# RWKV side work of the middle pairs four places earlier, VectorE's scan and gates two steps later beside head seven

## The chip, the cores and the metric

The kernel runs on one core of one Trainium2 chip. The metric is the device time of one execution in microseconds (us); lower is better. Engines are named PE (TensorE, the matmuls), DVE (VectorE), ACT (ScalarE), POOL (GpSimd) and SP (SyncE, which here only issues transfers). Each engine works through its own instructions strictly in the order in which the program lists them and waits on semaphores where it needs another engine's result.

## The reference

One layer of a streaming encoder, 1024 positions of width 1024, in float32:

```python
h = x
proj = rms_norm(h, mix_norm) @ w_in_first
att = mla_group(proj[..., :MLA_COLS], ...)            # 8 heads, chunk-causal softmax attention
rw, _ = rwkv7_group(token_shift(proj[..., MLA_COLS:], mu), ...)   # 8 heads of 64
h = h + concatenate([att, rw]) @ w_out
h = h + mem_cross_attention(rms_norm(h, ca_norm), mem_n, ca_wq, ca_wkv, ca_wo)
h = h + squared_relu_mlp(rms_norm(h, mlp_norm), mlp_w_up, mlp_w_down)
return rms_norm(h, final_norm)
```

The part that matters here is the recurrence inside `rwkv7_group`, which runs strictly forward in time for each head:

```python
sa = einsum('bhvk,bhk->bhv', state, at)
state = state * wt[:, :, None, :] + sa[..., None] * bt[:, :, None, :] + vt[..., None] * kt[:, :, None, :]
y = einsum('bhvk,bhk->bhv', state, rt)
```

The decay `wt`, the removal vector `at`, its partner `bt` and the mixed key `kt` are made from the projection by low-rank products, tanh, exp, a norm over each head and a running sum of the log decay over time. Afterwards each head's `y` is normalized, gets a bonus term and is multiplied by a gate.

## The kernel before

**Stages.** The projection comes first, then the eight attention heads (outer loop `h` over heads, inner loop `q` over eight query windows of 128), then the RWKV loop, then the output projection, cross-attention and the MLP. Head seven is `h == BESIDE`, that is `h = 6`.

**RWKV loop.** The eight RWKV heads are worked in four pairs, `p = 0` to 3 (the text calls them first to fourth pair). In a pair the 1024 positions are 16 chunks of 64 in four groups `g`. A group begins with `solve` (PE L1433), `local` and `carry` (L1455 to L1492), and then has four steps `k`, one for each chunk `c`: PE makes the next state (`st`, L1512), DVE copies it out of PSUM (L2856), and PE makes the outputs (L1525). State `c + 1` needs the copy of state `c`. At the head of a group, the states need `mt`, a DVE sum (L2846). Also in the steps, PE works ahead for the next group: `double_q`, `double_z` (L1408 to L1422, with DVE's L2819 and L2828 behind them), `scores` (L1366, L1368, DVE's L2702 behind them), `tokens` (L1379 to L1382, ACT's copies behind them) and at the end `a_v` (L1395), which needs the state copy of the group's last chunk.

**Side work.** Between these steps stands side work: `prep(p + 1)`, which makes the next pair's inputs, and `post(p - 1)`, which finishes the previous pair's output. Each is cut into numbered slots; a slot may have instructions on PE, ACT and DVE. The RWKV loop has numbered places, 4 to 47 in each pair: places `11g + 4` to `11g + 6` stand in the head of group `g`, places `11g + 7 + 2k` and the one after it in step `k`. Before the change place `s` does slot `s`, and places 44 to 47 do slots 0 to 3 of the pair after next:

```python
def place_of(p, s):
    return (p, s) if s < SLOTS else (p + 1, s - SLOTS)
```

`beside(p, s)` on PE, ACT and DVE calls this. POOL and SP have their own order.

**Slots by name (DVE line in brackets).** 0 and 2: low-rank products on PE (L1237), tanh on ACT. 3: `kk`, `t1p` and the scan `L` (L2584, L2587, L2592). 4: `na`, `am` (L2595, L2598). 5: `k2` (L2601), and on ACT the squares `kksq` (L1964). 6 and 7: head sums on PE (L1240, in later pairs L1247), their logarithms on ACT (L1970, L1974). 10 to 12: exponentials on ACT. 14: `nkk` (L2604). 15: `at` (L2609). 16: `b`, `bt` (L2614, L2618). 17: `kt` (L2621). 18 and 19: `al` on PE (L1303), which needs `bt`, and its copy on DVE (L2631). 21: `rk` (L2638). 24: two memsets. 26 to 30: the substitution, 30 small operations in a chain (L2654, L2657) and a copy. 33 and 34: bonus sums (PE L1247, DVE L2667, L2671). `post` is 22 slots later: 24 the squares and 28 the head sums of y, 37 `yn`, `yb`, 38 and 39 the gate (PE L1237, DVE L2696).

**The transfer chain.** When slot 19 is done, SP stores the `al` blocks to HBM and loads them back as `sc_s`; the substitution waits for that load. After it SP stores the result and loads it into `H`; the next pair's first `double_q` (PE L1408) waits for that. SP's `inverse` and `blocks` issue these in a fixed order.

**Head seven.** Beside each `q` of heads seven and eight stand slots of `prep(0)`; `beside_heads` lists them. DVE does them after the maximum (`row_max`, L2534) of that `q`; the next `q`'s maximum comes after them. ACT's exponential and PE's transposes (L1182) wait for the maximum.

Of the kernel before, what the change touches and what calls it, by code (L numbers as in the profile page):

```python
# [19 lines left out]
NW = S // P  # L20
# [11 lines left out]
PAIRS = 4  # L32
# [84 lines left out]
BESIDE = 6  # L117
SLOTS = 44
POST = 22
RP_SET = 6  # L120
# [48 lines left out]
def build(nc, x_t, mem_t, pos, wall, vecs, con_d, headw, wv_d, lora_d, out_t):  # L169
    with ExitStack() as ctx:  # L170
# [291 lines left out]
        for g in range(SLOT_END):  # L462
            n, part, j = part_of(g)
# [124 lines left out]

        def place_of(p, s):

            return (p, s) if s < SLOTS else (p + 1, s - SLOTS)

        def beside_heads(h, q):

            i = 9 * (h - BESIDE) + q
            if h < BESIDE:
                return ()
            if i < 9:
                return ((0,), (1,), (2,), (3, 4), (5, 6), (7, 8, 9), (10, 11), (12, 13, 14), (15, 16, 17))[i]
            return ((), (18,), (19, 21, 22), (24,), (26, 27), (28, 29, 30), (33,), (34,), ())[i - 9]  # L600

        mm_act, mm_dve, mm_pe = sem("mem_act"), sem("mem_dve"), sem("mem_pe")
# [356 lines left out]
        def _(pe):  # L959
# [569 lines left out]
            def beside(p, s):  # L1529
                p, s = place_of(p, s)  # L1530
                if p == PAIRS:
                    return
                if p >= 1:
                    post(p - 1, s - POST)
                else:
                    attention_end(s)
                if p < PAIRS - 1:
                    prep(p + 1, s)
                elif s == 9:
                    memory_sums()  # L1540
# [292 lines left out]
        def _(act):  # L1833
# [209 lines left out]
            def beside(p, s):  # L2043
                p, s = place_of(p, s)
                if p == PAIRS:
                    return
                if p >= 1:
                    post(p - 1, s - POST)
                if p < PAIRS - 1:
                    prep(p + 1, s)  # L2050
                else:
                    memory_step(s)
# [334 lines left out]
        def _(dve):  # L2387
# [182 lines left out]
            def prep(n, s):  # L2570
# [10 lines left out]
                if s == 3:  # L2581
                    if n >= 1:
                        r_at(P_ACT, f"afirst_{n - 1}")
                    r(nc.vector.tensor_scalar(rKK, kk_, vec[:, V_KK + n:V_KK + n + 1], -1.0, ALU.mult, ALU.mult), "kk")  # L2584
                if s == 3:
                    r_at(P_ACT, f"tw1_{n}")
                    r(nc.vector.tensor_scalar(rT1, rT1, 1.0, None, ALU.add), "t1p")  # L2587
                if s == 3:
                    own("t1p")
                    if n == 0:  # L2590
                        dve.wait_ge(step_made, 3)
                    r(nc.vector.tensor_tensor_scan(rWi, rStep, rT1, 0.0, ALU.mult, ALU.add), "L")  # L2592
                if s == 4:
                    r_at(P_ACT, f"ta1_{n}")
                    r(nc.vector.tensor_scalar(rA, rA, -0.5, -0.5, ALU.mult, ALU.add), "na")  # L2595
                if s == 4:
                    own("na")
                    r(nc.vector.tensor_scalar(rT1, rA, 1.0, vec[:, V_KA + n:V_KA + n + 1], ALU.add, ALU.mult), "am")  # L2598
                if s == 5:
                    own("am")  # L2600
# [105 lines left out]
            def beside(p, s):  # L2706
                p, s = place_of(p, s)
                if p == PAIRS:
                    return
                if p >= 1:  # L2710
# [61 lines left out]
            for h in range(MLA_HEADS):  # L2772
                for q in range(NW):
# [9 lines left out]
                    if q < NW - 1:  # L2783
                        filled(h, q)
                        for s in beside_heads(h, q):
                            prep(0, s)
                if h < MLA_HEADS - 1:
                    queries(h + 1)
                filled(h, NW - 1)
                for s in beside_heads(h, NW - 1):  # L2790
                    prep(0, s)
                filled(h, NW)
                if h == BESIDE - 1:
                    for u, half in UNFILLED:
                        evict_half(u, half)
                for s in beside_heads(h, NW):
                    prep(0, s)
# [477 lines left out]
```

## Time and profile before

| what | value |
|---|---|
| median of 3 runs | 1712.31 us (1707.43 to 1717.62) |
| profiled execution | 1711.84 us |
| its span | 1709.9 us |
| PE busy | 1637.6 us (96%) |
| DVE busy | 1119.9 us (65%) |
| ACT busy | 874.8 us (51%) |
| POOL busy | 769.2 us (45%) |
| chain that ended last | PE 75%, DVE 13%, issue 3%, ACT 3%, DMA 3% |

The span is the time from the first to the last instruction in the profile; the device time of the same execution is 1.9 us more. Busy time is the time in which an engine has an instruction in work. PE at 96% is the engine that sets the time; what it waits for and at which clock it runs is the place to look. In the lines below, a name such as `sa` or `PS` is a tensor, `PS` is PSUM.

### The profile page before, as it was taken

Reading aid. Unit: us, or ns where it says so; the run is one execution under the profiler, and the core shown is the slowest. Engines: PE = TensorE matmul, PEld = TensorE weight load, DVE = VectorE, ACT = ScalarE, POOL = GpSimd, SP = SyncE. Lnnn points to the kernel's source line nnn. Section 1 sums busy time; section 2 is a strip of 40 time slices with the busy share of each in tenths; the row PEclk is TensorE's granted clock in tenths of the full one; section 3 lists DMA queues with packets and bytes.
Section 4 is the critical chain, followed back from the end, with each engine's and each line's share of the span. In section 5 each row is a group of like instructions: output and inputs, shape, how many; then the busy total and the mean of one; then the engine's idle time right before and its main releaser. Section 6 shows DMA issues by size and latency. Waiting matters only on the chain.

```text
span 1709.9 us, 30411 instructions
## 1 busy us (share of the span) xinstructions
PE 1637.6 (96%) x11876; PEld 1270.0 (74%) x11876; DVE 1119.9 (65%) x1732; ACT 874.8 (51%) x1695; POOL 769.2 (45%) x555
## 2 busy tenths in 40 slices
PE   8999999988888889899999999999999999999997
PEld 6676777745577677688977667788888888888886
DVE  7744343435576775633787769887758856784788
ACT  5323233345425455511463467776667666656763
POOL 4210212011212012322492266877768695867771
PEclk9999999988999999999999999999999999999999
DMA  6100010001122222422302002020211203020202
GB/s 243 37 26 22 25 47 1 22 6 31 33 37 46 50 47 106 160 87 74 112 28 72 1 7 93 25 75 25 75 41 59 73 27 99 26 74 26 74 1 99
DMA packets 82842, 94.47 MB, mean 55 GB/s; under 512 B 53776, under 2 KB 56336, under 8 KB 82704
## 3 DMA queue, kind: packets, MB, share of 16 engines
q1 hardware_dynamic: 82704, 92.57, 17.3%
q8 instruction: 94, 1.54, 0.4%
q14 instruction: 44, 0.36, 0.1%
HBM read 82.57 MB, written 9.98 MB: 54 GB/s over the span
## 4 chain that ended last, share of the span: by engine, by line
PE 75%; DVE 13%; issue 3%; ACT 3%; DMA 3%; POOL 2%; SPq 1%; DVEq 0%; ACTq 0%; POOLq 0%
PE PS L1779 39%; PE PS L1063 8%; PE PS L978 5%; PE PS L1164 3%; PE PS L1203 2%; PE PS L1182 2%; PE PS L1735 2%; PE PS L1713 1%; PE PS L1566 1%; PE PS L1237 1%; DVE H L2993 1%; POOL sa L926 1%; DVE sa L2919 1%; DVE sc_s L2654 1%; DVE sc_s L2657 1%
## 5 line engine op out<-in xcount | busy, mean ns | idle before, releaser
L1779 PE MATMUL PS<-memr,wsp 128*128 128x512 f32 x1488 | 357.5, 391 | 1.1 <-DVE memr L2975 1.1
L1779 PEld LDWEIGHTS PS<-memr,wsp 128*128 128x128 f32 x1488 | 278.7, 188 | 63.2 <-DVE memr L2975 3.2
L941 POOL TENSOR_TENSOR wsp<-sa,wsp 128x512 fp32r<-128x512 f32 x120 | 164.4, 1373 | 167.9 <-ACT wsp L2227 167.7
L1779 PE MATMUL PS<-memr,wraw_r 128*128 128x512 f32 x744 | 180.1, 390 | 0.5 <-DVE memr L2975 0.5
L1779 PEld LDWEIGHTS PS<-memr,wraw_r 128*128 128x128 f32 x744 | 139.4, 188 | 31.1 <-DVE memr L2975 1.2
L1779 PE MATMUL PS<-tmp_r,wsp 128*128 128x512 f32 x564 | 147.2, 395 | 3.7 <-DVE tmp_r L2975 3.4
L1063 PE MATMUL PS<-xn,wsp 128*128 128x512 f32 x576 | 146.3, 400 | 2.5 <-DVE proj L2450 1.6
L2975 DVE TENSOR_TENSOR memr<-PS,memr 128x512 fp32r<-128x512 f32 x185 | 126.0, 681 | 34.2 <-ACT PS L2265 34.2
L832 POOL CAST wsp<-wraw 128x1024 fp32r<-128x1024 f32 x24 | 28.0, 1166 | 238.3 <-PE PS L1063 112.6
L2993 DVE TENSOR_TENSOR H<-PS,H 128x512 f32<-128x512 f32 x160 | 108.0, 686 | 39.7 <-PE PS L1779 24.3
L1914 ACT ACTIVATE H<-PS,mst 128x128 f32<-128x128 f32 (+3 forms) x64 | 47.5, 742 | 165.8 <-DVE mst L2534 165.8
L1063 PEld LDWEIGHTS PS<-xn,wsp 128*128 128x128 f32 x576 | 104.4, 188 | 35.3 <-issue 15.8
L1779 PEld LDWEIGHTS PS<-tmp_r,wsp 128*128 128x128 f32 x564 | 105.4, 188 | 29.4 <-DVE tmp_r L2975 5.1
L2256 ACT CAST memr<-sa 128x512 fp32r<-128x512 f32 x114 | 70.3, 616 | 109.9 <-PE PS L1779 77.1
L941 POOL TENSOR_TENSOR wraw_r<-sa,wraw_r 128x512 fp32r<-128x512 f32 x64 | 88.9, 1393 | 53.4 <-ACT wraw_r L2227 53.4
L978 PE MATMUL PS<-xn,wsp 128*128 128x512 f32 x480 | 109.9, 390 | 1.1 <-issue 1.1
L926 POOL TENSOR_TENSOR sa<-sa 128x512 f32<-128x512 f32 x64 | 93.0, 1456 | 34.3 <-DMA sa<-in_weights_dram 32.5
L978 PEld LDWEIGHTS PS<-xn,wsp 128*128 128x128 f32 x480 | 90.0, 188 | 20.6 <-issue 1.9
L2534 DVE TENSOR_REDUCE mst<-PS 128x1 f32<-128x128 f32 (+3 forms) x64 | 48.1, 753 | 86.3 <-PE PS L1167 86.1
L2265 ACT COPY PS<-sa 128x512 f32<-128x512 f32 x175 | 102.0, 583 | 3.1 <-DVE con_r L2975 1.8
L2919 DVE TENSOR_TENSOR sa<-sa 128x512 f32<-128x512 f32 x80 | 94.7, 1187 | 6.6 <-ACT sa L2206 6.6
L941 POOL TENSOR_TENSOR wsp<-sbx,wsp 128x512 fp32r<-128x512 f32 x66 | 88.7, 1346 | 10.9 <-ACT wsp L2227 10.9
(394 smaller groups left out, 3420.0 us busy)
## 6 DMA issues: line engine op xcount, KB each, us to landing
sa<-in_weights_dram SPq DMA_DIRECT2D x40, 512.0 KB, 4.3
wraw<-in_weights_dram SPq DMA_DIRECT2D x24, 512.0 KB, 3.8
sa<-in_weights_dram SPq DMA_DIRECT2D x48, 256.0 KB, 2.7
H<-in_x_dram SPq DMA_DIRECT2D x16, 512.0 KB, 7.7
sbx<-in_weights_dram SPq DMA_DIRECT2D x32, 256.0 KB, 2.8
H<-in_weights_dram SPq DMA_DIRECT2D x8, 512.0 KB, 6.9
out_dram<-sbx SPq DMA_DIRECT2D x16, 256.0 KB, 2.1
a_dram<-H SPq DMA_DIRECT2D x16, 128.0 KB, 2.5
```

The costliest lines, as they stand in the source:

```text
L926: nc.gpsimd.tensor_tensor(out, a, b, op).then_inc(W_SUM.sem, W_SUM.one(name))
L941: nc.gpsimd.tensor_tensor(w[:, 1, :], w_source(g), w[:, 0, :].bitcast(F32), ALU.subtract).then_inc(mw_rest, 1)
L978: last = nc.tensor.matmul(PS[:, bank + half, :], wsp[:, k, kt, a, :], src[:, at, b, HALF * half:HALF * half + HALF], start=(i == 0 and (a, ...
L1063: last = nc.tensor.matmul(PS[:, bank, :], wsp[:, u % 2, kt, a, :], xn[:, kt, b, HALF * half:HALF * half + HALF], start=(kt == 0 and (a, b) ...
L1164: nc.tensor.matmul(PS[:, b + part, 0:n], mQ[:, win(q)], mK[:, HALF * part:HALF * part + n], start=True, stop=(part < q // 4))
L1779: last = nc.tensor.matmul(PS[:, bank_of(g), :], w[:, a, win(k)], x[:, b, :], start=(k == 0 and (a, b) == (0, 0)), stop=(k == ROWS - 1 and ...
L2256: nc.scalar.copy(x_split_of(d)[:, 0, :], x_source(d)).then_inc(mx_head, 1)
L2265: nc.scalar.copy(PS[:, PS_BANKS + d % 2, :], x_source(d)).then_inc(mx_staged, 1)
L2534: m(nc.vector.tensor_reduce(mNeg[h % 2][:, q:q + 1], two(2 * (q % 2))[:, 0:P * (q + 1)], AX_X, ALU.max, negate=True), f"m{h}_{q}")
L2919: nc.vector.tensor_tensor(out, a, b, op).then_inc(X_SUM.sem, X_SUM.one(name))
L2975: nc.vector.tensor_tensor(x[:, 1, :], source, x[:, 0, :].bitcast(F32), ALU.subtract).then_inc(mx_rest, 1)
L2993: out(nc.vector.tensor_tensor(tile, a, b, ALU.add), f"{kind}{part}_{v}")
```

## The change

`AHEAD = 4` moves the side work of the RWKV loop forward. In the second and third pair every place does the slot four further on. In the first pair the lead grows from 0 to 4: places 13, 22, 31 and 40 do two slots each. In the first two pairs the last four places, 44 to 47, then do slots 4 to 7 of the pair after next, where they did 0 to 3. In the third pair places 40 to 43 are empty and 44 to 47 do slots 0 to 3 of the last pair's side work, as before. The last pair is unchanged, and so are POOL and SP.

Beside head seven, DVE's slot 3 keeps only `kk`; `t1p` and the scan go from `q = 3` to `q = 4`, and `na`, `am` and `k2` to `q = 5`.

```diff
 SLOTS = 44
+AHEAD = 4
 POST = 22
 RP_SET = 6
...
 
-        def place_of(p, s):
-
-            return (p, s) if s < SLOTS else (p + 1, s - SLOTS)
+        def reached(p, s):
+
+            if p == PAIRS - 1:
+                return s
+            return s + (min(AHEAD, max(s - 4, 0) // 9) if p == 0 else AHEAD)
+
+        def slots_at(p, s):
+
+            last = reached(p, s)
+            first = last if s <= 4 else reached(p, s - 1) + 1
+            slots = [(p, x) for x in range(first, last + 1) if x < SLOTS]
+            if p == PAIRS - 2:
+                return slots + [(p + 1, s - SLOTS)] * (s >= SLOTS)
+            return slots + [(p + 1, x - SLOTS) for x in range(first, last + 1) if x >= SLOTS]
...
+
+        def vector_beside_heads(h, q):
+
+            if h == BESIDE and 3 <= q <= 5:
+                return ((3,), (4,), (5, 6, 7, 8, 9))[q - 3]
+            return beside_heads(h, q)
...
 
             def beside(p, s):
-                p, s = place_of(p, s)
-                if p == PAIRS:
-                    return
+                for pair, slot in slots_at(p, s):
+                    if pair < PAIRS:
+                        beside_slot(pair, slot)
+
+            def beside_slot(p, s):
                 if p >= 1:
...
                     r(nc.vector.tensor_scalar(rKK, kk_, vec[:, V_KK + n:V_KK + n + 1], -1.0, ALU.mult, ALU.mult), "kk")
-                if s == 3:
+                late = 0 if n else 1
+                if s == 3 + late:
                     r_at(P_ACT, f"tw1_{n}")
                     r(nc.vector.tensor_scalar(rT1, rT1, 1.0, None, ALU.add), "t1p")
-                if s == 3:
+                if s == 3 + late:
                     own("t1p")
                     if n == 0:
                         dve.wait_ge(step_made, 3)
                     r(nc.vector.tensor_tensor_scan(rWi, rStep, rT1, 0.0, ALU.mult, ALU.add), "L")
-                if s == 4:
+                if s == 4 + late:
                     r_at(P_ACT, f"ta1_{n}")
                     r(nc.vector.tensor_scalar(rA, rA, -0.5, -0.5, ALU.mult, ALU.add), "na")
-                if s == 4:
+                if s == 4 + late:
                     own("na")
                     r(nc.vector.tensor_scalar(rT1, rA, 1.0, vec[:, V_KA + n:V_KA + n + 1], ALU.add, ALU.mult), "am")
-                if s == 5:
+                if s == 5 + late:
                     own("am")
                     r(nc.vector.scalar_tensor_tensor(rT1, rT1, 1.0, kk_, ALU.subtract, ALU.mult, reverse0=True), "k2")
...
                     if q < NW - 1:
                         filled(h, q)
-                        for s in beside_heads(h, q):
+                        for s in vector_beside_heads(h, q):
                             prep(0, s)
```

The same `beside` is put into PE's, ACT's and DVE's program. Line numbers of the changed kernel are some 22 to 25 higher on DVE.

DVE beside head seven, before, from the output sum of `q = 3` on (L2534 is a maximum, L2543 the output sum, the `sa` rows are slots 3, 4 and 5):

```order
L2543 TENSOR_TENSOR mO_odd<-PS,mO_odd 64x256
L2584 TENSOR_SCALAR sa<-proj,vec 128x1024
L2587 TENSOR_SCALAR sa<-sa 128x1024
L2592 SCALAR_TENSOR_TENSOR sa<-step,sa 128x1024
L2595 TENSOR_SCALAR sa<-sa 128x1024
L2598 TENSOR_SCALAR sa<-sa,vec 128x1024
L2534 TENSOR_REDUCE mst<-PS 128x1
L2601 SCALAR_TENSOR_TENSOR sa<-sa,proj 128x1024
L2534 TENSOR_REDUCE mst<-PS 128x1
```

And after (L2556 is the maximum, L2565 the output sum):

```order
L2565 TENSOR_TENSOR mO_odd<-PS,mO_odd 64x256
L2606 TENSOR_SCALAR sa<-proj,vec 128x1024
L2556 TENSOR_REDUCE mst<-PS 128x1
L2610 TENSOR_SCALAR sa<-sa 128x1024
L2615 SCALAR_TENSOR_TENSOR sa<-step,sa 128x1024
L2556 TENSOR_REDUCE mst<-PS 128x1
L2565 TENSOR_TENSOR mO_odd<-PS,mO_odd 64x256
L2618 TENSOR_SCALAR sa<-sa 128x1024
L2621 TENSOR_SCALAR sa<-sa,vec 128x1024
L2624 SCALAR_TENSOR_TENSOR sa<-sa,proj 128x1024
L2556 TENSOR_REDUCE mst<-PS 128x1 x2
```

Five operations stood ahead of the maximum of `q = 4`; now only one does, and three stand ahead of the maximum of `q = 6`.

DVE in the second pair, steps `k = 2` and 3 of the first group up to the `mt` of the second, before (L2856 the state copy, L2604 `nkk`, L2846 `mt`):

```order
L2856 COPY tmp<-PS 64x128
L2819 TENSOR_TENSOR sc_w<-PS,con 128x128 x2
L2856 COPY tmp<-PS 64x128
L2828 TENSOR_TENSOR H<-PS,H 128x128 x2
L2604 SCALAR_TENSOR_TENSOR sa<-sa 128x1024
L2609 TENSOR_TENSOR sa<-sa 128x8x2x63
L2614 TENSOR_TENSOR sa<-sa 128x1024
L2618 TENSOR_TENSOR sa<-sa 128x1024
L2846 TENSOR_TENSOR ssum<-PS,ssum 128x2x2x128
L2621 TENSOR_TENSOR proj<-sa 128x1024
L2856 COPY tmp<-PS 64x128
```

And after (L2881 the state copy, L2627 `nkk`, L2632 `at`, L2637 and L2641 `b` and `bt`, L2644 `kt`, L2654 the copies of `al`, L2871 `mt`):

```order
L2725 TENSOR_TENSOR sc_w<-PS,con 128x384
L2627 SCALAR_TENSOR_TENSOR sa<-sa 128x1024
L2881 COPY tmp<-PS 64x128
L2844 TENSOR_TENSOR sc_w<-PS,con 128x128 x2
L2632 TENSOR_TENSOR sa<-sa 128x8x2x63
L2637 TENSOR_TENSOR sa<-sa 128x1024
L2641 TENSOR_TENSOR sa<-sa 128x1024
L2881 COPY tmp<-PS 64x128
L2853 TENSOR_TENSOR H<-PS,H 128x128 x2
L2644 TENSOR_TENSOR proj<-sa 128x1024
L2654 TENSOR_TENSOR H<-PS,con 128x4x64 x4
L2871 TENSOR_TENSOR ssum<-PS,ssum 128x2x2x128
```

`nkk` went ahead of the state copy of step 2, `at`, `b` and `bt` went ahead of the copy of step 3, and `kt` and the four `al` copies ahead of `mt`.

DVE at the end of the second pair, steps 2 and 3 of its last group, before (L2584, L2587, L2592 are `kk`, `t1p` and the scan):

```order
L2702 TENSOR_TENSOR sc_w<-PS,con 128x384
L2856 COPY tmp<-PS 64x128
L2819 TENSOR_TENSOR sc_w<-PS,con 128x128 x2
L2828 TENSOR_TENSOR H<-PS,H 128x128 x2
L2584 TENSOR_SCALAR sa<-proj,vec 128x1024
L2587 TENSOR_SCALAR sa<-sa 128x1024
L2592 SCALAR_TENSOR_TENSOR sa<-step,sa 128x1024
L2595 TENSOR_SCALAR sa<-sa 128x1024
L2598 TENSOR_SCALAR sa<-sa,vec 128x1024
```

And after (L2606, L2610 and L2615 are `kk`, `t1p` and the scan, L2618 to L2624 are `na`, `am`, `k2`):

```order
L2725 TENSOR_TENSOR sc_w<-PS,con 128x384
L2606 TENSOR_SCALAR sa<-proj,vec 128x1024
L2610 TENSOR_SCALAR sa<-sa 128x1024
L2615 SCALAR_TENSOR_TENSOR sa<-step,sa 128x1024
L2881 COPY tmp<-PS 64x128
L2844 TENSOR_TENSOR sc_w<-PS,con 128x128 x2
L2618 TENSOR_SCALAR sa<-sa 128x1024
L2621 TENSOR_SCALAR sa<-sa,vec 128x1024
L2624 SCALAR_TENSOR_TENSOR sa<-sa,proj 128x1024
L2853 TENSOR_TENSOR H<-PS,H 128x128 x2
L2871 TENSOR_TENSOR ssum<-PS,ssum 128x2x2x128
```

The scan and the two operations ahead of it went ahead of the state copy of step 2. The end of the first pair has the same order.

## Rows read from the trace of the kernel before

**Rows 1.** Windows, RWKV loop: busy us and count per engine, PEclk, DMA share, GB/s

```profile
460.00:705.00 245.00, 214.29 (x4950) 169.19 (x4946) 171.78 (x414) 119.72 (x280) 54.51 (x48) 0.97 0.25 63
```

**Rows 2.** Timeline, head seven: start us, us, engine, line, operation [idle before it <- releaser]

```profile
372.33 0.73 DVE L2584 TENSOR_SCALAR sa<-proj,vec 128x1024 f32<-128x1024 f32 x1
...
373.14 0.19 PE L1167 MATMUL PS<-mask_row 128*128 128x64 bf16 x1
...
373.70 2.29 DVE L2592 TENSOR_TENSOR_SCAN sa<-step,sa 128x1024 f32<-128x1024 f32 x1
...
377.28 0.81 DVE L2534 TENSOR_REDUCE mst<-PS 128x1 f32<-128x640 f32 x1
...
380.50 2.08 PE L1240 MATMUL PS<-sa,con 128*128 128x512 f32 x2 [6.42 <-ACT sa L1964]
...
382.37 2.52 PE L1164 MATMUL PS<-H 128*128 128x512 f32 x4
```

**Rows 3.** Windows, two stretches at the lower clock, columns as in rows 1

```profile
378.00:384.50 6.50, 4.00 (x5) 1.85 (x6) 1.23 (x2) 5.47 (x7) 0.00 (x0) 0.50 0.00 0
...
562.00:569.00 7.00, 5.18 (x84) 4.64 (x88) 5.65 (x23) 1.29 (x2) 0.16 (x1) 0.51 0.27 33
```

**Rows 4.** Waits of PE in the RWKV loop: us in total, times, longest us

```profile
PE PS L1512 <- DVE tmp L2856: 8.1, 7, 1.9
PE PS L1512 <- DVE ssum L2846: 7.1, 4, 2.5
PE PS L1247 <- ACT sa L1964: 2.4, 3, 1.0
PE PS L1408 <- DMA H<-xt_dram: 2.0, 1, 2.0
PE PS L1433 <- ACT sc_s L2040: 1.8, 3, 0.8
...
PE PS L1303 <- DVE H L2631: 1.4, 3, 0.5
PE PS L1512 <- ACT sc_s L2026: 1.1, 3, 0.4
```

**Rows 5.** Timeline, second pair, substitution on DVE and a wait of PE behind it

```profile
556.45 0.18 DVE L2654 TENSOR_TENSOR sc_s<-sc_s 128x15 f32<-128x15 f32 x1 [2.84 <-DMA sc_s<-a_dram]
...
563.82 0.55 PE L1512 MATMUL PS<-tmp,ssum 128*64 128x64 f32 x3 [1.91 <-DVE tmp L2856]
```

**Rows 6.** Chain that ended last, second pair: start us, us, what

```profile
533.37 0.32 PE PS L1512 x3
...
535.84 0.61 PE PS L1408 x16
...
568.15 0.87 PE PS L1408 x14
```

**Rows 7.** Timeline, second pair, first group: DVE and PE

```profile
535.43 0.56 DVE L2702 TENSOR_TENSOR sc_w<-PS,con 128x384 f32<-128x384 f32 x1
...
538.51 1.22 DVE L2604 SCALAR_TENSOR_TENSOR sa<-sa 128x1024 f32<-128x1024 f32 x1
...
538.89 0.87 PE L1395 MATMUL PS<-sc_s,sc_w 64*64 64x64 f32 x16
...
543.28 0.68 DVE L2846 TENSOR_TENSOR ssum<-PS,ssum 128x512 f32<-128x512 f32 x1
```

**Rows 8.** Timeline, turn from pair to pair: DVE, PE and ACT

```profile
589.20 2.29 DVE L2592 TENSOR_TENSOR_SCAN sa<-step,sa 128x1024 f32<-128x1024 f32 x1
...
586.59 1.70 PE L1237 MATMUL PS<-proj,sc_s 32*128 32x512 f32 x4
...
594.50 1.09 PE L1247 MATMUL PS<-sa,con 64*64 64x512 f32 x8 [1.01 <-ACT sa L1964]
...
530.47 1.28 ACT L1970 ACT_TABLE_LOAD   x1
532.39 1.21 ACT L1974 ACTIVATE sa<-PS 64x512 f32<-64x512 f32 x2
```

More of the change, by code:

```diff
@@ L2043, in beside, with beside_slot @@
             def beside(p, s):
-                p, s = place_of(p, s)
-                if p == PAIRS:
-                    return
+                for pair, slot in slots_at(p, s):
+                    if pair < PAIRS:
+                        beside_slot(pair, slot)
+            def beside_slot(p, s):
                 if p >= 1:
@@ L2706, in beside, with beside_slot @@
             def beside(p, s):
-                p, s = place_of(p, s)
-                if p == PAIRS:
-                    return
+                for pair, slot in slots_at(p, s):
+                    if pair < PAIRS:
+                        beside_slot(pair, slot)
+            def beside_slot(p, s):
                 if p >= 1:
@@ L2789, in _ @@
                 filled(h, NW - 1)
-                for s in beside_heads(h, NW - 1):
+                for s in vector_beside_heads(h, NW - 1):
                     prep(0, s)
@@ L2795, in _ @@
                         evict_half(u, half)
-                for s in beside_heads(h, NW):
+                for s in vector_beside_heads(h, NW):
                     prep(0, s)
```

## The prediction

> **What bounds the kernel now.** PE sets the time, so I read its waits first, then the timeline around each long one, then the windows for the clock. In the RWKV loop of 245 us PE is busy 214 us at a mean granted clock of 0.97 [rows 1]. The waits there are short and many [rows 4]. The largest are PE's states waiting for DVE: 8.1 us for the state copy and 7.1 us for `mt`. They are longest behind the substitution, whose 30 small operations stand in front of those copies: in the second pair the substitution begins at 556.45, after DVE itself has waited 2.84 us for the load of `sc_s`, and a state waits 1.91 us until 563.82 [rows 5]. So the side work costs time where a block of DVE work is longer than the PE work beside it, and the question is what stands beside each block after the move.
>
> Head seven shows the same thing at its largest. The maximum of `q = 4` could run at 373.3, when the scores end (L1167 at 373.14); it runs at 377.28, behind `kk`, `t1p`, the scan of 2.29 us, `na` and `am`. PE then waits 6.42 us for `kksq` on ACT, which stands behind the exponential of that maximum [rows 2].
>
> **Head seven.** After the change only `kk` (0.73 us from 372.33) stands ahead of that maximum: it starts at about 373.4, 3.9 us earlier, and the exponential, `kksq` and PE's L1240 follow it. In the trace PE's granted clock is 0.50 of full from 378.0 to 384.5 [rows 3], which is the 1.2 GHz level, and began some 4 us into that idle time. With the idle time 3.9 us shorter I expect no fall there: L1240 takes 2.08 us at that clock and would take half, and L1164 2.52 us would lose about a third; at 0.8 of that, since both overlap with ACT work, it is 1.1 us. Against it, `na` and `am` (375.99 to 377.28, 1.3 us) and `k2` (1.2 us, taken as L2604 of the same size [rows 7]) now stand ahead of the maximum of `q = 6`; ACT is busy with logarithms and a table load there, and I count 0.4 us. Sum: -3.9 - 1.1 + 0.4 = **-4.6 us**. Bounds: -2 if the clock falls anyway and the late gates hold the maximum fully, -6 if they cost nothing. Everything up to the RWKV loop is then earlier by that much, since PE, ACT and DVE go through head eight in the same order as before.
>
> **RWKV loop, what is removed.** In the first three pairs:
> - the states behind the substitution: three waits of 1.9 for the copy, 5.7 us, and three of the four for `mt`, 7.1 - 1.4 (the one at the start of the loop, which stays) = 5.7 us [rows 4];
> - the lower clock behind them. In the second pair the granted clock is 0.51 from 562 to 569 [rows 3]. From the state of step 1 to the next `double_q` PE takes 535.84 - 533.37 = 2.47 us in a group at full clock and 568.15 - 563.82 = 4.33 us there [rows 5, 6], so 1.9 us lost to the lower clock. I take the same for the third pair, which has the same order and the same waits, and 1.2 as an estimate for the first, where the last places differ: 5.0 us;
> - `al` waiting for the copy of the first half (1.4), vector copies on ACT (1.1), two of the three waits for `kksq` (1.4), the wait for `H` at the start of the second pair (2.0), two of three waits of L1433 (0.9) [rows 4], and in two turns the low-rank products that wait for ACT's tanh and take 1.70 us instead of 1.1 [rows 8]: together 8.0 us.
> Sum: **24.4 us**, if all of it goes.
>
> **What is added.** Each wait is counted by laying DVE's operations one behind the other in the new order, with PE's steps beside them at their durations.
> - *`bt` ahead of `al`, second and third pair.* DVE is free at 536.0 (L2702, 535.43 + 0.56). `nkk`, the copy and masks of step 2, then `at`, `b`, `bt`: four operations of 1.2 (`nkk` to `bt` fill 538.51 to 543.28 without a gap) and 0.7 us end at 541.4. PE has done step 3 by 539.15, a little after today's `a_v` at 538.89 [rows 7]; its next instruction is now `al`, which needs `bt`. That is 2.2 us, plus 0.3 for the copy of step 2. Today the same four run beside `a_v`, `solve` and `local`, which is their cover; PE has 4.9 us of work there.
> - *`rk` directly behind `mt`*: 1.28 us ahead of a state copy, 0.6 us seen, and 0.2 for the memsets.
> - *Substitution.* Seven places lie between `al` and slot 26 as before, so the load lands within half a microsecond of where DVE asks for it, 5.9 us behind `mt`. Slots 26 and 27 take 3.8 us (16 operations of 0.2 and their gaps, from 556.45 on) and stand in step 2, so the copy of step 3 is done at 10.0. PE, whose four steps take 7.3 us and with `post`'s head sums 8.4, is then at `a_v`, which needs that copy: 1.6 us. `mt` waits 0.2 more for slots 28 to 30.
> - *Bonus sums* in steps 0 and 1 of the third group: 0.8. *`yn`, `yb` and the gate* in steps 2 and 3: 1.0.
> Together 6.9 us in each of the two pairs, **13.8**.
> - *Turns after the first and second pair.* The scan (2.29 us [rows 8]) with `kk` and `t1p`, 3.6 us, stands ahead of the state copy of step 2, and PE's last output needs that copy: 2.7 us. Then `kksq`, the head sums (1.09 us [rows 8], moved from the start of the next pair, so no new work) and ACT's logarithms come ahead of ACT's `a_v` copies: the 1.21 us of L1974 [rows 8] hold `solve` by 1.1, and 0.1 more for the masks. 3.9 us each, **7.8**.
> - *First pair.* The lead is small; `al` is done only 0.5 us earlier, but the substitution is asked for one place sooner than that, so DVE waits some 3.7 us for the load (2.84 in the second pair today [rows 5]), and 28 of the 30 operations, 6.5 us, stand ahead of `mt`. From there PE has 5.5 us of work (the rest of step 3, `a_v`, `solve`, `local`): 3.7 + 6.5 - 5.5 = 4.7 us for `mt`, and 1.5 in small ones, **6.2**. The stored result is then some 2 us earlier, so the wait of PE for `H` goes.
> Sum: 27.8 us. **Clock**: the 4.7 us wait is like the 6.42 us one that was followed by the low clock, 1.9 us; of the two turns, with waits of 2.7 and 1.1 close together as behind the substitution today (1.7 and 1.9), I count one, 1.9 us. Together 31.6. Loop: 31.6 - 24.4 = **+7.2 us**. Its bounds are -15 (the moved DVE work finds cover at all the new places) and +14 (twice the clock loss and the load 1 us late in each pair).
>
> The Trainium skill ("ScalarE: Activation LUTs", What ACT_TABLE_LOAD costs) puts a switch of tables at about 2.7 us, of which 1.3 is the load and the rest a drain. In this trace the load takes 1.28 us, to 531.75, and the second of the two logarithms behind it starts at 532.39, so that there is no room for a drain of that length [rows 8]. By the page each turn would cost 1.4 us more, 2.8 in all; the sum goes by the row.
>
> POOL and SP keep their order. POOL's `rt`, `kh` and `bh` wait for exponentials and `rk` that now come earlier; behind them on POOL stands the next group's diagonal, which is needed only at `mt`. SP waits for `al` and the substitution, both earlier, so nothing queued behind them gets later. The last pair and all behind it keep their durations.
>
> **Sum.** 1711.8 (the profiled execution, 0.5 us under the median of the runs) - 4.6 + 7.2 = **1714.4 us**.
>
> **The rivals.**
> - *The moved work is covered* (faster, 0.20). DVE runs beside PE, and where PE's own steps last longer than I count, the blocks of 1.2 us fit. For it: DVE has long idle stretches in the pair's last group today, and 11.4 us of substitution waits do go. Against it: the state copies are in DVE's own queue, so any backlog shows. Without the `bt` waits (5.0) and the turns (7.8), and with only one stretch of low clock, the loop is at 27.8 - 12.8 + 1.9 - 24.4 = -7.5, the whole at 1699.7.
> - *Only head seven counts* (0.15). What goes and what comes in the loop cancel to a microsecond or two: 1707 to 1708.
> - *The clock falls behind each new wait* (slower, 0.15). New idle times of 2 to 5 us at five places (first pair's `mt`, two `al`, two turns) with the lower level after each, at 1.9 us as in the second pair or at 3.4 us, half of a stretch of nearly 7 us: 9.5 to 17 us in place of the 3.8 counted. With 13.5 it is 1724. It decides once the loop has lost 13 us against before, since 4.6 come back in head seven. The Trainium skill ("TensorE: Matmul & The Clock Gate", HAM oscillation) describes such a fall behind each wait as the usual case in thin loops. By rows, the wait of 2.0 us for `H` is not followed by one, the pairs of waits behind the substitution are.
> - *Forecast*: gain in head seven, a somewhat larger loss in the loop (0.50), 1708 to 1720.
>
> **How the numbers follow.** About 0.5% (8.6 us) is what a measurement here can tell from no change. The covered case is faster in nine of ten (0.18), the head-seven case in one of seven (0.02), the forecast in one of fifty (0.01): 0.21. The clock case is slower in nine of ten (0.135) and the forecast in one of nine (0.055): 0.19. The rest, 0.60, is within it. The range reaches into both outer cases: 1701 to 1723. The forecast's own is 1708 to 1720.
>
> **What would show it.** Head seven: the maximum of `q = 4` right behind `kk`, PE's wait for `kksq` near 3 us or less, no low clock there; DVE's maximum of `q = 6` right behind `k2`. Loop: waits of PE for `mt` and the state copy down to about a third in the second and third pair; a new wait of L1303 for `bt` of 2 us in each; a wait of L1525 for the state copy behind the scan in two turns; one of `solve` for ACT; a long `mt` wait in the first pair; no wait for `H`. I am wrong if the `al` products do not wait for `bt`, if the low clock is gone from the loop, or if it is there in more than three stretches.

## The result and the profile after

| kernel | median us (range, runs) | ratio to before | 95% interval |
|---|---|---|---|
| before | 1709.88 (1707.15 to 1717.62, 7) | | |
| changed | 1727.86 (1722.66 to 1732.57, 7) | 1.0102 | 1.008 to 1.0123 |
| changed, measured again beside before at 1711.25 | 1725.69 (1720.64 to 1729.68, 6) | 1.0087 | 1.0067 to 1.0106 |

The change makes the kernel 0.9 to 1.0% slower, 15 to 18 us, where I forecast no measurable change at 1714 us. The profiled execution takes 1728.79 us at a span of 1726.8.

First the windows of the changed kernel: the RWKV loop, and then eight stretches inside it (columns as in rows 1).

```profile
460.00:720.00 260.00, 218.46 (x4914) 174.04 (x4907) 167.19 (x412) 119.76 (x278) 49.84 (x45) 0.93 0.24 59
...
498.00:504.50 6.50, 5.83 (x71) 4.00 (x72) 3.98 (x11) 0.00 (x0) 1.18 (x2) 0.50 0.36 43
525.00:528.00 3.00, 2.90 (x28) 1.47 (x28) 2.93 (x6) 1.66 (x2) 0.00 (x0) 0.50 0.03 5
545.50:548.50 3.00, 3.00 (x46) 2.87 (x42) 1.22 (x3) 1.30 (x5) 0.00 (x0) 0.50 0.02 5
562.50:569.00 6.50, 5.99 (x141) 5.88 (x143) 3.92 (x19) 2.22 (x7) 0.00 (x0) 0.50 0.17 22
597.00:600.00 3.00, 3.00 (x28) 1.39 (x28) 2.93 (x6) 1.66 (x2) 0.00 (x0) 0.50 0.02 5
617.50:620.50 3.00, 3.00 (x45) 2.87 (x42) 1.02 (x3) 1.38 (x5) 0.00 (x0) 0.50 0.02 5
634.50:637.50 3.00, 2.87 (x38) 2.76 (x41) 2.62 (x13) 1.18 (x4) 0.00 (x0) 0.50 0.00 0
661.50:664.50 3.00, 3.00 (x38) 2.44 (x31) 1.42 (x4) 0.00 (x0) 0.00 (x0) 0.50 0.34 135
```

The mean clock of the loop fell from 0.97 [rows 1] to 0.93. Before, three stretches in the loop were at the 1.2 GHz level, 17 us in all; now there are eight, 34 us in all. More than three was one of my signs of being wrong.

Second the waits of PE in the loop (us in total, times, longest), which answer to rows 4.

```profile
PE PS L1543 <- DVE tmp L2881: 6.9, 3, 2.8
PE PS L1413 <- DVE tmp L2881: 5.3, 2, 2.8
PE PS L1530 <- DVE ssum L2871: 5.3, 3, 4.4
PE PS L1530 <- DVE tmp L2881: 4.9, 9, 0.8
PE PS L1321 <- issue: 4.0, 2, 2.0
PE PS L1451 <- ACT sc_s L2060: 3.3, 3, 1.2
PE PS L1255 <- DVE proj L2719: 2.4, 3, 1.1
...
PE PS L1384 <- issue: 1.6, 1, 1.6
```

The names have moved by some twenty lines: L1543 is the last output, L1413 `a_v`, L1530 a state, L1321 `al`, L1451 `solve`, L1255 the gate. Those of 2 us and more each have a low stretch beginning in them or within a microsecond behind them, as PE's timeline shows (idle time before it in brackets):

```profile
498.44 0.69 PE L1530 MATMUL PS<-tmp,ssum 128*64 128x64 f32 x4 [4.41 <-DVE ssum L2871]
...
525.10 0.48 PE L1543 MATMUL PS<-sc_s,tmp 128*64 128x64 f32 x4 [2.76 <-DVE tmp L2881]
...
544.43 0.76 PE L1321 MATMUL PS<-sa 64*64 64x64 f32 x19 [2.01 <-issue]
...
563.01 1.12 PE L1413 MATMUL PS<-sc_s,sc_w 64*64 64x64 f32 x16 [2.76 <-DVE tmp L2881]
```

The third is named "issue", but DVE's `bt` (L2641) ends at 544.32, so it is the wait for `bt`. The same three come again in the third pair at 596.95, 616.24 and 634.63.

Third head seven, to be held against rows 2: DVE's maximum, its scan behind it, and PE's head sums and scores.

```profile
373.88 0.82 DVE L2556 TENSOR_REDUCE mst<-PS 128x1 f32<-128x640 f32 x1 [0.31 <-PE PS L1185]
...
375.34 2.29 DVE L2615 TENSOR_TENSOR_SCAN sa<-step,sa 128x1024 f32<-128x1024 f32 x1
...
377.11 1.12 PE L1258 MATMUL PS<-sa,con 128*128 128x512 f32 x2 [2.52 <-ACT sa L1984]
...
378.07 2.68 PE L1182 MATMUL PS<-H 128*128 128x512 f32 x4
```

This part did what it should: the maximum starts 3.4 us earlier, PE waits 2.52 us and not 6.42.

Last, where the time went by position. The 16 operations that write `mt`, one in each group, mark the loop; a line per kernel, before and then changed, has their first and last start:

```profile
L2846 DVE TENSOR_TENSOR ssum<-PS,ssum x16: 680/687/694, 466.4 to 699.2; 128x512 f32<-128x512 f32 x16
```

```profile
L2871 DVE TENSOR_TENSOR ssum<-PS,ssum x16: 682/692/693, 464.6 to 714.7; 128x512 f32<-128x512 f32 x16
```

Before the loop 1.8 us are won, in the loop from 232.8 to 250.1 us 17.3 are lost, and 1.4 behind it. From pair to pair (first `mt` to next first `mt`) the loss is 5.9, 8.1 and 3.8 us. A second profile of the changed kernel (second row of the table above) begins the loop at 461.5, 4.9 us earlier than before, and takes 252.4 us from first to last `mt`; its low stretches in the loop are eight again, 41 us.

### The profile page after: what moved, and what is told of

It reads as the page before. It is cut to its first block, busy times and chain, and to the rows that moved or that the text cites. A ratio compares the mean times of both kernels' runs of the same rounds, so it can differ in the third digit from the quotient of the medians.

```text
span 1726.8 us, 30411 instructions
## 1 busy us (share of the span) xinstructions
PE 1648.6 (95%) x11876; PEld 1279.9 (74%) x11876; DVE 1118.8 (65%) x1732; ACT 875.4 (51%) x1695; POOL 767.5 (44%) x555
## 4 chain that ended last, share of the span: by engine, by line
PE 78%; DVE 12%; issue 3%; ACT 3%; DMA 2%; POOL 1%; SPq 0%; DVEq 0%; ACTq 0%; POOLq 0%
PE PS L1799 39%; PE PS L1081 8%; PE PS L996 5%; PE PS L1182 3%; PE PS L1221 2%; PE PS L1200 2%; PE PS L1755 2%; PE PS L1586 1%; PE PS L1733 1%; PE PS L1255 1%; PE PS L1451 1%; POOL sa L944 1%; DVE xn L2427 1%; DMA sc_s<-a_dram 1%; PE PS L1141 1%
## 5 line engine op out<-in xcount | busy, mean ns | idle before, releaser
L2556 DVE TENSOR_REDUCE mst<-PS 128x1 f32<-128x128 f32 (+3 forms) x64 | 48.1, 753 | 81.9 <-PE PS L1185 81.8
```

The lines of the kernel that those rows point to most:

```text
L2556: m(nc.vector.tensor_reduce(mNeg[h % 2][:, q:q + 1], two(2 * (q % 2))[:, 0:P * (q + 1)], AX_X, ALU.max, negate=True), f"m{h}_{q}")
```

## The experiments

In the table "12 mt" is the time from the first pair's first `mt` to the third pair's last in the profiled execution, "16 mt" that to the last one of all. All kernels were timed beside the kernel before on their chip; ratios with 95% intervals. The "mt" columns come from one profile per kernel; the two of the changed kernel differ by 2 us in them.

| kernel | ratio to before | 12 mt us | 16 mt us |
|---|---|---|---|
| before | 1 | 175.9 | 232.8 |
| changed (two measurements) | 1.0102, 1.0087 | 191.4, 193.5 | 250.1, 252.4 |
| head seven part alone | 0.9979 (0.9966 to 0.9993) | 175.3 | 232.0 |
| loop part alone | 1.0088 (1.0067 to 1.0109) | 191.0 | 247.9 |
| changed, 178 dummies | 1.0121 (1.0103 to 1.0138) | 200.4 | 256.8 |
| changed, 88 dummies | 1.0042 (1.0026 to 1.0058) | 180.8 | 244.1 |
| before, head seven part and dummies | 0.9953 (0.9934 to 0.9971) | 169.8 | 227.4 |
| the same, ten more in head seven | 0.9962 (0.9942 to 0.9982) | 171.7 | 231.3 |
| changed, late scan in all turns | 1.0026 (1.001 to 1.0043) | 185.5 | 242.7 |
| the same with dummies | 1.0013 (0.9999 to 1.0026) | 181.3 | 239.0 |
| loop part alone, late scan | 1.0062 (1.0047 to 1.0077) | 182.5 | 241.8 |
| lead only in the first pair's last group | 1.0067 (1.0046 to 1.0088) | 189.5 | 247.9 |
| three places ahead | 1.0024 (1.0008 to 1.0041) | 182.6 | 239.6 |
| two places ahead | 0.9992 (0.9979 to 1.0005) | 176.7 | 232.7 |
| two places, dummies | 0.9982 (0.9965 to 0.9999) | 172.2 | 233.5 |
| two places, dummies, late scan | 0.9971 (0.9952 to 0.9989) | 171.6 | 230.6 |

**The two parts apart.** Edits: one kernel has only the changes around `late` and `vector_beside_heads`; the other has `late = 0` and `beside_heads` in their place.

> The kernel before with only the head seven part of the change (VectorE's scan, na, am and k2 one step later for the first tile); the RWKV loop as before. Both theories: PE's wait for the head sums near 2.5 us in place of 6.42, the low clock there about half as long, the first RWKV scores 3.7 us earlier. My forecast was 4.6 us. If the gain is kept to the end: 1705 to 1707 us, 3 to 5 under the kernel before. If it is lost again in a new stretch of low clock before the RWKV loop, as the trace of the whole change suggests (a gain of 3.7 us at the first scores, 1.8 at the first mt): 1707 to 1709.

> The changed kernel without the head seven part: only the places of the RWKV side work move. If the two parts are independent, the loop's loss stands alone: 18 + 2 to 4 = 20 to 22 us over the kernel before, 1730 to 1732 us. If the head seven part had shifted work against work in the loop and made the loss itself, this is well below: under 1722.

Head seven alone gives 3.6 us by its ratio (1.2 to 5.8 by the interval). That is a gain kept, 3 to 5 us, by the ratio, but the median of 1708.45 and the lower end of the interval would do for a gain partly lost, so the run does not decide between the two. The loop part alone costs 15 us (11 to 19), less than the 20 to 22 expected. The sum of the two, 1.0067, lies below the first measurement of the whole. The second was made to see this, and its interval begins there:

> The changed kernel itself, beside the others on one chip, and as a second profile of it. If the two parts of the change add up (1.0088 for the loop's move alone, 0.9979 for head seven alone), its ratio is 1.0067; the first measurement gave 1.0102. Near 1.010 again: head seven's 3.6 us are not kept in front of the changed loop. In the profile the waits come out within 0.3 us of the first; the stretches at half clock may shift by a few us and be 3.4 or 6.8 long.

So no interaction of the parts is shown.

**Waits or clock?** The waits can't be removed without removing the change, but PE's idling can. The edit, at the places where the changed kernel waits (lines of the second of the two runs, the one with 88 dummies):

```
+            def keep_warm(bank, n):
+                for _ in range(n):
+                    nc.tensor.matmul(PS[:, bank, 384:512], con[:, 0:P], con[:, 0:P], start=True, stop=True)
...
+                        if p in (0,) and g == 2 and k == 0:
+                            keep_warm(2, 18)
                         if c < NC - 1:
                             state(p, c)
                         if k > 0:
+                            if p < 2 and c == NC - 1:
+                                keep_warm(1, 11)
                             outputs(p, c)
```

and the like ahead of `al`, `a_v` and `solve`.

> The changed kernel with dummy matmuls of 128 columns (into unused columns of PSUM, results never read) in front of the new waits of PE: al in the second and third pair, mt in the first, the last output of the first two pairs, the copy before a_v and the solve after it. They end within the wait, so the waits stay and only PE's idling goes. Theory 'clock' (most of the unforeseen loss is the lower clock that follows each new wait): the five or more new stretches of low clock in the loop go, 1719 to 1722 us, 6 to 9 under the changed kernel. Theory 'waits' (the loss is the length of the waits, and the low clock falls where PE is not the bound): 1727 to 1730, no less than the changed kernel.

This run missed, by my count of a dummy. Its profile (PE's timeline) has the 36 dummies of the first pair's `mt` as one row, two instructions for each:

```profile
487.63 8.30 PE L1400 MATMUL PS<-con 128*128 128x128 f32 x72
```

That is 0.23 us each, so they did not end within the waits. They also stood ahead of `double_q` there. Although the mean clock of the run's loop was 0.99, it was as slow as the changed kernel or slower. With half the number, and in front of the state:

> As the run before it with dummy matmuls, but with half as many: there one dummy took 0.23 us and not the 0.11 counted, so that 178 of them stood in waits of 21.8 us for about 40 us. Now 18 ahead of the first pair's mt (directly in front of the state), 11 at each last output and each copy ahead of a_v, 8 at each al, 5 at each solve, so that they end within the waits. Theory 'clock': the loop from the first mt to the last, 250.1 us in the changed kernel, takes 236 to 241, the whole 1714 to 1718 us. Theory 'waits': loop 249 to 251, the whole 1726 to 1729.

The ratio fell from 1.0087 or 1.0102 to 1.0042, 8 to 10 us, and the loop to 244.1 us: most of what theory "clock" expected, but short of its 1718 and 241 us. The control does the same to the waits behind the substitution in the kernel before:

> The kernel before with the head seven part of the change and with dummy matmuls in the two waits behind the substitution, in each of the first three pairs: 8 ahead of the state that waits for mt, 7 ahead of the state that waits for the first state copy. The waits stay. Theory 'clock': the three stretches of 6.8 us at half clock go, 1.9 to 3.4 us each, 6 to 10 us together: 1699 to 1703 us, loop from first to last mt 222 to 226 in place of 232. Theory 'waits': 1707 to 1710.

It gained 0.26% over the head seven part alone, 4.5 us, under the 6 to 10 expected (the two intervals still overlap by 0.0005), and has **the lowest ratio of the study: 1705.24 us against 1711.83**, better than both before and changed; two other kernels with dummies, at 0.9962 and 0.9971, can't be told from it. The windows of the first three pairs of four kernels, before, changed, changed with dummies, and before with head seven part and dummies:

```profile
466.40:642.30 175.90, 154.09 (x3552) 121.70 (x3552) 126.86 (x324) 80.98 (x197) 31.42 (x31) 0.95 0.23 45
```

```profile
464.60:656.00 191.40, 158.77 (x3558) 126.55 (x3558) 124.65 (x325) 82.70 (x199) 31.38 (x31) 0.92 0.23 48
```

```profile
465.70:646.40 180.70, 166.55 (x3732) 136.62 (x3732) 125.08 (x324) 82.10 (x199) 31.39 (x31) 1.00 0.23 48
```

```profile
465.30:635.10 169.80, 159.18 (x3650) 127.06 (x3645) 126.07 (x324) 81.85 (x199) 31.41 (x31) 1.00 0.22 44
```

The last two are both at full clock, so their difference of 10.9 us is waits alone. The clock is worth 191.4 - 180.7 = 10.7 us in the changed kernel and 175.3 - 169.8 = 5.5 us in the one it is compared with: 5.2 us of the change's 16.1 in this stretch. (The filled waits may end some tenths later than the empty ones; that would make the share of waits a little smaller.) By the second profile of the changed kernel (193.5) it is 12.7 for the clock, so 7.2 of 18.2. Neither theory holds alone: about two thirds are waits, a third or a little more is clock. By the ratios, with dummies in both kernels the change still costs 0.89%, 15 us, where it costs 18 to 21 without them; 5.7 of the 15 are lost in the fourth pair (63.3 against 57.6 us from the third pair's last `mt` to the last one), where PE stops with nothing to wait for, as the last section tells.

Ten more dummies in head seven's wait gave nothing:

> The kernel before with the head seven part, dummy matmuls in the two waits behind the substitution, and ten more in PE's wait for kksq in head seven. Against the run without those ten (0.9953): the stretch of 3.4 us at half clock at 379 goes, up to 1.7 us, so 0.9943 to 0.9953, 8 to 10 us under the kernel before, if the clock is what counts there; no gain if ACT is the bound of that stretch.

**Which block.** The scan first, one slot later in all turns (`late = 1`):

> The changed kernel with the late scan for all tiles: t1p, scan, na, am and k2 one slot later in the turns of the loop too, so that the scan stands behind the state copy of step 2 and not ahead of it. Theory 'waits': the two waits of 2.76 us for the last output of a pair go, 1722 to 1723 us. Theory 'clock': the stretches of 3.4 us at half clock behind them go as well, 1.7 each, 1719 to 1721. Rival: the scan only moves to stand ahead of another copy, and PE waits there: 1726 to 1730.

> The changed kernel with the late scan in all turns (1714.1 us) and half as many dummy matmuls as in the first such run, ahead of mt in the first pair, al, the copy ahead of a_v and solve. Theory 'clock': its four stretches of low clock in the loop (20.5 us) go, 7 to 10 us: 1704 to 1708 us. Theory 'waits': 1713 to 1716.

> The loop's move with the late scan in all its turns, head seven as before. Against the same with head seven (1.0026): 1.0047 if head seven's gain is kept, 8 us over the kernel before; 1.0020 to 1.0030 if it is lost. Against the loop's move alone (1.0088): the late scan takes 7 us or more off, which is more than the two waits of 2.76 us, if the low clock behind them is part of their price; 5 to 6 us by the waits alone.

The waits of 2.76 us for the last output are gone in all three, as expected. Without dummies the late scan gives 10 to 13 us with head seven's part (over what I expected) and 4.5 without it. The last kernel's 1.0062 is compatible with the 1.0047 expected only at the edge of its interval.

The kernel with dummies missed what "clock" expected: 1713.94 us, in the range of "waits" and not 1704 to 1708. Against the late scan without dummies its ratio fell by 0.13%, 2 us, and its "12 mt" by 4.2 us. Against the changed kernel with dummies the ratio is 0.29% lower, 5 us, which looks like the length of the two waits but is not: "12 mt" is the same (181.3 against 180.8), and in the profiles the gain lies in the fourth pair (57.7 against 63.3), where the order is the same. What the late scan is worth is better read in a turn, from a pair's last `mt` to the next pair's first. The windows of the second turn in the loop part alone, then with the late scan, then the changed kernel with dummies, then with late scan and dummies:

```profile
586.31:606.09 19.78, 15.68 (x312) 10.66 (x310) 10.63 (x20) 10.34 (x23) 1.18 (x2) 0.91 0.01 2
```

```profile
586.94:603.75 16.81, 14.44 (x312) 10.15 (x310) 10.53 (x21) 10.13 (x23) 1.18 (x2) 1.00 0.01 3
```

```profile
580.66:599.10 18.44, 18.04 (x344) 13.86 (x345) 10.63 (x21) 10.24 (x23) 1.18 (x2) 1.00 0.01 3
```

```profile
577.72:594.80 17.08, 15.83 (x322) 11.46 (x322) 10.53 (x20) 10.13 (x23) 1.18 (x2) 1.00 0.01 3
```

With the clock free the turn gets 3.0 us shorter (the first turn 3.1, 20.4 to 17.2), with the clock full 1.4: of the 2.76 us some come back as a wait of 0.9 for `kksq`, and about half of the turn's gain is clock. The two turns make some 6 us, between the 4.5 and the 10 to 13 of the ratios.

Nor is each wait followed by low clock. With the late scan in the changed kernel, the third pair's `al` and `a_v` wait as before, and the clock stays full from 560.5 to 706 (PE's timeline, then a window):

```profile
605.44 1.05 PE L1321 MATMUL PS<-sa 64*64 64x64 f32 x29 [2.02 <-issue]
...
623.00 0.68 PE L1413 MATMUL PS<-sc_s,sc_w 64*64 64x64 f32 x16 [2.25 <-DVE tmp L2881]
```

```profile
600.00:640.00 40.00, 31.91 (x744) 25.34 (x740) 31.49 (x86) 15.94 (x41) 6.28 (x7) 1.00 0.28 50
```

In the second pair the same two waits do have low stretches at them, 536 to 543.5 and 556.5 to 560.5:

```profile
536.04 1.64 PE L1321 MATMUL PS<-sa 64*64 64x64 f32 x29 [2.01 <-issue]
...
556.31 0.79 PE L1413 MATMUL PS<-sc_s,sc_w 64*64 64x64 f32 x16 [2.92 <-DVE tmp L2881]
```

Then the lead itself, `AHEAD = 2` and `AHEAD = 3`, and the lead of the first pair taken late, with `max(s - 31, 0) // 3` for `max(s - 4, 0) // 9`:

> The changed kernel with the side work two places ahead in place of four. If each place costs alike: half the loss, 1717 to 1720 us. If the loss hangs on which block stands ahead of which copy (the scan ahead of the state copy of step 2, bt ahead of al, the substitution ahead of the third state copy): with two places those three fall elsewhere, and it can be anywhere from 1706 to 1725; then the waits of PE name the place.

> The changed kernel with the side work three places ahead. Two places cost nothing (0.9992), four cost 15 to 18 us (1.0087 and 1.0102). Theory 'blocks': the loss comes with named waits, so this run has some of them whole and others not at all, and its time is the number of them times 2 to 5 us each: with bt ahead of al but neither the scan ahead of the last output nor the substitution ahead of a_v, 1.001 to 1.004. Theory 'even': each place alike, 1.004 to 1.006 with waits of half their length.

> The changed kernel with the lead of the first pair taken in its last group only (places 34, 37, 40 and 43) in place of one in each nine from place 13. By my term the first pair loses 6.2 us through the wait of 4.7 for mt and small ones; here that wait should be near the 2.0 of the kernel before and 5 to 7 us come back, less what four jumps in one group cost: ratio 1.006 to 1.008. Rival: the lead has to be made up somewhere, and DVE's blocks of 1.2 us stand closer ahead of the copies of the last group: no gain, 1.009 to 1.012.

Two places cost nothing, three cost 4 us, four 15 to 18. In the profile of two places there is no wait for `bt`, none for the last output and none for `a_v`; it has instead longer waits for `mt` (both in PE's timeline):

```profile
558.27 0.45 PE L1530 MATMUL PS<-tmp,ssum 128*64 128x64 f32 x4 [2.66 <-DVE ssum L2871]
...
621.67 0.64 PE L1530 MATMUL PS<-tmp,ssum 128*64 128x64 f32 x4 [3.42 <-DVE ssum L2871]
```

At three places the wait for the last output is still missing, the one for `bt` is partly there, and the one for `a_v` partly in the second pair (below) and wholly in the third (2.55 us):

```profile
541.12 1.05 PE L1321 MATMUL PS<-sa 64*64 64x64 f32 x29 [0.85 <-issue]
...
555.90 0.68 PE L1413 MATMUL PS<-sc_s,sc_w 64*64 64x64 f32 x16 [1.74 <-DVE tmp L2881]
```

The ratio of 1.0024 is what "blocks" expected, but the waits are not all whole or missing: each comes in at its own lead, some in part, and the scan's needs the fourth place. The late lead of the first pair brings its `mt` wait from 4.55 to 2.27 us, as expected, and the ratio to 1.0067, within the 1.006 to 1.008 expected; against 1.0087 on the same chip that is 3.4 us and not 5 to 7, and the two intervals overlap so far that no gain is not excluded. In the profile its first three groups take about what they took before (47.2 against 46.7 us), and the fourth 19.7 us against 17.5.

**Clock at two places.**

> The changed kernel two places ahead, with 17, 10 and 13 dummy matmuls in the waits for mt of the first three pairs (4.28, 2.66 and 3.42 us, which were followed by three stretches of low clock, 17 us). The waits stay. Theory 'clock': 4 to 8 us under the same kernel without them (0.9992), so 0.9945 to 0.997; theory 'waits': 0.998 to 1.000.

> As the run before it, with the late scan in all turns. At two places the scan stands ahead of no copy that PE waits for, so it should change nothing: within 0.0015 of the run before it. A gain of 3 us or more would say that the late scan's effect in the changed kernel (1.0026 against 1.0087 to 1.0102) is not by the two waits of 2.76 us.

The dummies bring 4.5 us up to the third pair's last `mt` (176.7 to 172.2), as "clock" has it, but only 0.1% in all: the ratio of 0.9982 is in the range of "waits". In the profile the rest is lost in the fourth pair (61.3 against 56.1 us), in stops told of in the last section. The late scan changes 0.1%, within what it should be.

**The price of the low clock.** Four pairs of kernels differ by dummies alone. In the first three pairs 30.6 us at half clock went from the changed kernel and gave 10.7 us; 20.4 went from the kernel with head seven's part and gave 5.5; 17.0 with the late scan gave 4.2; 13.6 at two places gave 4.5. (The lengths are read off windows of half a microsecond.) So one microsecond at half clock cost 0.25 to 0.35 us here.

## Why the prediction was wrong

*Head seven, -4.6 us: right in its mechanism, a little too large.* The maximum starts 3.4 us earlier (I had 3.9), and the half-clock stretch shrank from 6.8 to 3.4 us but did not go (I had it gone). Alone it gives 3.6 us. In the profile of the whole change, PE's first RWKV scores are 3.8 us earlier and the first `mt` only 1.8: 2.0 us were given back before the loop, where a stretch at half clock from 453.2 to 460.1 stands that the kernel before does not have. The second profile has only half of that stretch and keeps 4.9 us, so that it isn't shown that the change makes this loss.

*What the loop loses in waits: right, one by one, where a wait has a name of its own.* First pair's `mt` 4.7 against 4.41 measured, last outputs 2.7 against 2.76, `bt` 2.2 against 2.01, `solve` 1.1 against 1.24, gate 1.0 against 1.09, no wait for `H`. Only `a_v` was short: 1.6 against 2.76 and 2.57, 2.1 us over two pairs. My net for the waits was 27.8 less 19.4 (the 24.4 without the 5.0 of clock), 8.4 us; at full clock the first three pairs show 10.9. "`bt` ahead of `al`" and "the scan ahead of the last output" were thus foreseen to a quarter of a microsecond.

*What the loop loses in clock: the step that failed.* "The 4.7 us wait is like the 6.42 us one that was followed by the low clock, 1.9 us; of the two turns [...] I count one, 1.9 us" made 3.8 us added against 5.0 removed. Removed was right (5.5 by the control). Added was 10.7. The price of the low clock was near: 10.7 us for 30.6 us of it, 0.35 us each, where my 1.9 for a stretch of 6.8 is 0.28. The number of stretches was the fault: I counted two, and in these three pairs there were seven. I had counted low clock behind a wait only if the wait was long or two stood close together, and leaned on the one wait of 2.0 us for `H` that had none behind it. In the changed kernel the waits of 2.0 for `bt` and of 2.76 for the last output each had one behind them, both times that they occur. (Why a wait of 2 us is followed by one in one place and not in another, as in the third pair with the late scan, no run tells.) This is the rival "the clock falls behind each new wait", with 9.5 to 17 us, to which I gave 0.15. The Trainium skill ("TensorE: Matmul & The Clock Gate", HAM oscillation) describes such a loss at each step of a loop with some 2 us of matmuls between waits of 3 to 5 us for DMA. The trace agrees that it comes again and again, in eight stretches, but here seven of them stand at waits of 2.0 to 4.4 us for DVE.

*Not in the prediction at all:* 1.7 us in the fourth pair, where its order is as before, of which 1.58 is one stop of PE at L1384; and 1.4 us behind the loop, where a half-clock stretch is 6.8 us long and not 3.4. The second profile has the first of the two (1.9) and not the second.

The sum: 1714.4 + 2.8 (head seven: -4.6 against -1.8) + 6.4 (clock: 10.7 - 5.5 against 3.8 - 5.0) + 2.5 (waits) + 1.7 + 1.4 is 1729.2, against 1728.8 profiled. It goes by one profile; in the second the kernel wins 3.1 us more ahead of the loop, loses 2.3 more in it and 2.2 less behind it. The loop's own bound of +14 us, which allowed for twice the 3.8 us of clock, was passed with 17.3. The range ended at 1723, short even of that rival's own 1724, since I let it hold no more than its chance; 6.9 us more of clock than counted and 2.5 of waits led over it.

## What to carry to other kernels

A wait of 2 us on the engine that sets the time can cost twice: once as itself and once as the half clock that may follow, at 0.25 to 0.35 us for each at half clock here. Where a change trades a few long waits for more short ones, count the clock for each of them, and put a bound on it by their number and not by the stretches there are today. Such waits can be filled: 45 dummy matmuls in two waits of each of the first three pairs gave 4.5 us here, though 66 gave 2 us in another kernel and 40 less than 2 in a third. First measure one dummy: where the fill ended after the waits, the run was no faster than with empty ones. And where side work is moved against a loop, a sweep of the distance (two places free, three 0.24%, four 0.9 to 1.0%) tells more than the two ends.

## What the runs showed that I had not expected

**The same instructions before the loop come up to 6 us apart.** The changed kernel, its second measurement and its run with too many dummies have one order up to the loop, and the low stretches at other places. The first start of their `mt`, the number ahead of "to", is 464.6 (above), 461.5 and 458.8:

```profile
L2871 DVE TENSOR_TENSOR ssum<-PS,ssum x16: 684/692/694, 461.5 to 713.8; 128x512 f32<-128x512 f32 x16
```

```profile
L2891 DVE TENSOR_TENSOR ssum<-PS,ssum x16: 683/692/693, 458.8 to 715.5; 128x512 f32<-128x512 f32 x16
```

A single profile says nothing on gains under some 6 us ahead of the loop. The measured times of one kernel spread by up to 14 us (1704.15 to 1718.29 in the 29 runs of the kernel before beside the one three places ahead).

**PE stops with nothing to wait for, and in some kernels with dummies for longer.** In the fourth pair, the waits list has PE idle by "issue" for 0.6 us before, 1.6 in the changed kernel, and with dummies (changed with 88 dummies, then two places with dummies):

```profile
PE PS L1392 <- issue: 2.7, 1, 2.7
PE PS L1523 <- issue: 2.3, 1, 2.3
```

```profile
PE PS L1515 <- issue: 2.5, 2, 1.4
PE PS L1445 <- issue: 1.9, 1, 1.9
```

Half-clock stretches follow several of them, and the fourth pair takes up to 5 us longer than with empty waits (from the third pair's last `mt` 63.3 against 58.7, and 61.3 against 56.1). Neither the number of instructions nor PE's pace does it alone: with all 178 dummies the stops there are 0.2 us and the fourth pair takes 56.4, and the kernel with the shortest "12 mt" of all (169.8) has 0.7. My guess is that the supply of instructions falls behind; no run tests that, so the cause stays open.
